# S5 state inputs in four PSUM banks of their own, computed two pairs ahead, and streamed tiles in two banks

## The reference

```
bu_re = einsum('blgc,gnc->blgn', uf, bbar_re)      # 32 groups of 16 channels -> 64 states each
bu_im = einsum('blgc,gnc->blgn', uf, bbar_im)
_, _, s_re, s_im = lax.associative_scan(_complex_affine_combine, (abar_re, abar_im, bu_re, bu_im), axis=1)
y = einsum('blgn,gcn->blgc', s_re, c_re) - einsum('blgn,gcn->blgc', s_im, c_im) + d * uf
...
merged = gates[0] * (y_rw @ w_branch[0]) + gates[1] * (y_s5 @ w_branch[1]) + gates[2] * (y_gla @ w_branch[2])
```

## Time and profile before

| | us |
|---|---|
| median of 3 runs | 1868.67 |
| lowest, highest | 1866.36, 1868.9 |
| profiled execution | 1868.79 |
| its span | 1866.7 |
| TensorE busy in the span | 1766.2 (95%) |
| VectorE busy | 907.7 (49%) |
| ScalarE, GpSimd busy | 406.8, 295.9 |
| mean granted TensorE clock | 0.979 of full speed |

### The profile page before, as it was taken

How to read it: one execution, slowest core, us unless ns; L and a number is a source line. 1 busy time by engine, 2 the same in 40 slices (tenths; PEclk the granted TensorE clock), 3 DMA queues, 4 the chain that set the end, 5 groups by cost and what they waited for, 6 DMA issues and landing times.

```text
span 1866.7 us, 25902 instructions
## 1 busy us (share of the span) xinstructions
PE 1766.2 (95%) x10456; PEld 1393.1 (75%) x10456; DVE 907.7 (49%) x1725; ACT 406.8 (22%) x771; POOL 295.9 (16%) x305
## 2 busy tenths in 40 slices
PE   7999999899999999899899999988999899999997
PEld 5434454488888888656899996856798688888886
DVE  1247542464675444575587643187711432255511
ACT  1312453221012210346222002221421101200000
POOL 0100252122002211005233110066000000000000
PEclk9999999999999999999999999889999999999999
DMA  7775492122233222321345454232312343244443
GB/s 290 290 294 200 159 346 107 68 86 76 110 135 113 90 78 82 111 68 48 133 167 173 164 179 140 92 110 106 114 55 84 118 153 135 91 158 157 142 152 113
DMA packets 38703, 256.22 MB, mean 137 GB/s; under 512 B 4128, under 2 KB 7328, under 8 KB 9024
## 3 DMA queue, kind: packets, MB, share of 16 engines
q1 hardware_dynamic: 36240, 240.86, 36.6%
q0 software_dynamic: 1776, 9.57, 1.4%
q10 hardware_dynamic: 576, 4.19, 0.5%
HBM read 247.27 MB, written 7.34 MB: 136 GB/s over the span
## 4 chain that ended last, share of the span: by engine, by line
PE 80%; DVE 12%; ACT 2%; issue 2%; POOL 2%; DMA 2%; SPq 0%; ACTq 0%; DVEq 0%; POOLq 0%
PE ps L595 79%; DVE arena L1873 1%; PE ps L790 1%; DMA ring<-weights 1%; DVE arena L2031 1%; DMA xT<-x_t 1%; POOL aux L1676 0%; DVE aux L1903 0%; DVE arena L1904 0%; DVE arena L1905 0%; ACT hT L1322 0%; DVE arena L2070 0%; POOL aux L1659 0%; DVE spare L2143 0%; POOL hT L1719 0%
## 5 line engine op out<-in xcount | busy, mean ns | idle before, releaser
L595 PE MATMUL ps<-hT,ring 128*128 128x256 f32 (+3 forms) x3184 | 744.1, 392 | 22.6 <-issue 17.0
L595 PEld LDWEIGHTS ps<-hT,ring 128*128 128x128 f32 (+1 forms) x3184 | 574.6, 194 | 182.3 <-issue 112.6
L595 PE MATMUL ps<-arena,ring 128*128 128x256 f32 (+3 forms) x1884 | 380.4, 358 | 5.0 <-DVE arena L1905 3.2
L595 PEld LDWEIGHTS ps<-arena,ring 128*128 128x128 f32 (+1 forms) x1884 | 317.6, 190 | 59.0 <-issue 13.7
L1659 POOL TENSOR_TENSOR aux<-aux 128x256 f32<-128x256 f32 (+1 forms) x46 | 50.1, 1088 | 611.0 <-ACT aux L1257 542.9
L595 PE MATMUL ps<-arena,sums 128*128 128x256 f32 (+1 forms) x768 | 136.5, 327 | 1.3 <-DVE aux L1969 1.3
L595 PEld LDWEIGHTS ps<-arena,sums 128*128 128x128 f32 x768 | 118.2, 191 | 12.3 <-DVE aux L1969 2.5
L1257 ACT ACTIVATE aux<-xT 128x256 f32<-128x256 f32 (+1 forms) x64 | 30.9, 494 | 285.7 <-DVE xT L2061 93.3
L1676 POOL TENSOR_SCALAR aux<-aux,small 128x512 f32<-128x512 f32 (+1 forms) x48 | 70.9, 1485 | 113.6 <-DVE small L1921 113.4
L1695 POOL TENSOR_TENSOR arena<-arena 128x256 f32<-128x256 f32 (+1 forms) x32 | 27.0, 843 | 332.6 <-ACT arena L1442 332.6
L595 PE MATMUL ps<-hT,sums 128*128 128x128 f32 (+1 forms) x512 | 78.6, 302 | 0.7 <-DVE aux L1969 0.4
(11 more groups left out here) (335 smaller groups left out, 1817.1 us busy)
## 6 DMA issues: line engine op xcount, KB each, us to landing
ring<-weights SPq DMA_DIRECT2D x224, 1024.0 KB, 4.9
kept_turns<-aux ACTq DMA_DIRECT2D x4, 1024.0 KB, 5.6
arena<-kept_turns POOLq DMA_DIRECT2D x6, 512.0 KB, 4.9
kept_keys_values<-spare POOLq DMA_DIRECT2D x1, 2048.0 KB, 10.2
arena<-kept_keys_values POOLq DMA_DIRECT2D x1, 2048.0 KB, 8.2
tab<-tables SPq DMA_DIRECT2D x1, 1344.0 KB, 13.7
arena<-mem_t SPq DMA_DIRECT2D x2, 512.0 KB, 5.6
xT<-ctx_t SPq DMA_DIRECT2D x1, 1024.0 KB, 9.2
```

Of the source, the lines that this page charges most:

```text
L595: ins = nc.tensor.matmul(o_, lhsT, rhs, start=start, stop=stop, skip_group_check=True)
```

## The change

Only TensorE's program differs. The inputs `("bu", n)` are opened from a new pool `state` of banks 0 to 3: even pairs get banks 0 and 1, odd pairs banks 2 and 3. From `s5_in(0)` to the loop's end, everything else from the pool `run` (the two GLA outputs, `glago` 3, the rw tiles and three gate tiles) takes turns in banks 4 and 7. `s5_in(1)` stands ahead of the loop; inside, `s5_in(m + 2)` comes right behind `s5_out(m)`. After the loop `run` has six banks again, in another order.

```diff
-            turn = {"run": 0, "hold": 0, "mod": 0}
-            pools = {"run": [0, 1, 2, 3, 4], "hold": [5, 6], "mod": [7]}
+            turn = {"run": 0, "hold": 0, "mod": 0, "state": 0}
+            pools = {"run": [0, 1, 2, 3, 4], "hold": [5, 6], "mod": [7], "state": [0, 1, 2, 3]}
...
-                    open_bank(("bu", n))
+                    open_bank(("bu", n), "state")
...
+            pools["run"], turn["run"] = [4, 7], 0
             s5_in(0)
             taken(pe, ("gatt",))
...
+            s5_in(1)
             for m in range(S5T // 2):
-                if m + 1 < S5T // 2:
-                    s5_in(m + 1)
                 s5_filler(2 * m)
                 s5_out(m)
+                if m + 2 < S5T // 2:
+                    s5_in(m + 2)
                 s5_filler(2 * m + 1)
+            pools["run"] = [4, 7, 0, 1, 2, 3]
```

## The result

The changed kernel takes 1871.1 us (median of 18 runs, 1867.66 to 1874.42), the kernel before 1867.17 (18 runs, 1863.45 to 1871.73). The ratio is 1.0018 with a 95% interval of 1.0010 to 1.0025: +3.4 us, from 1.9 to 4.7. The forecast was 1870.6 within 1867.5 to 1874.0, and no change beyond 0.2% as the likeliest. The profiled execution has a span of 1869.2 us, 2.5 above the one before. The profiled executions are not equally typical: that of the kernel before (1868.79 us) lies 1.6 us above its median of 18, that of the changed kernel (1871.29) 0.2 above.

The account below looks back on a forecast made before the run. The S5 loop was taken as bound by a ring of states, rw tile 7 and VectorE, not by inputs; +0.6 at `s5_in(0)` and +1.15 at rw tile 13 gave +1.8, 1870.6 us, range 1867.5 to 1874.0.

Parts of the forecast that it names:

- either long idle time: TensorE's idle times ahead of `s5_out(2)` and `s5_out(4)`, forecast to stay near 7.8 and 5.8 us.
- rival C: Rw tile 3's addition misses its gap between GpSimd's operations, tile 4's is then unblocked: +0.4 us, 1869.2 us; chance 0.13.
- The waits for rw tiles 7 and 11: VectorE's waits for these tiles in the S5 loop, forecast to grow from 4.2 to 5.3 us.
- rival B: Low clock lasts longer behind the two restarts, with narrow `s5_in` first: +3.9 us, 1872.7 us; chance 0.25.
- 1.54 us at `s5_out(7)`: TensorE's idle time ahead of `s5_out(7)`, forecast to grow from 0.3 to about 1.5 us.
- the ring: The S5 loop's limit: states, then rw tile 7, then VectorE, then states; inputs computed earlier gain 0.
- Rival D: Inputs were the S5 loop's limit, so both long idle times vanish: -19 us, about 1850 us; chance 0.07.
- Wait of `s5_in(0)`, +0.6: `s5_in(0)` waits for bank 1 until ScalarE has read `glago` 2: +0.6 us, bounds 0.5 and 0.9.
- Place of `s5_in`: `s5_in` ahead of the odd rw tile: odd tiles end 1.06 us later, costing only +1.15 us at rw tile 13.
- my term: Cost of moving `s5_in` ahead of the odd rw tiles, all of it at rw tile 13: +1.15 us.
- The giving back behind rw tile 11: Rw tile 11 comes 1.06 us later, but tile 12's addition still ends at 1290.1: cost 0.
- the loss at rw tile 13: Rw tile 13's addition is held by GpSimd's operation and ends at 1295.4 instead of 1294.24: +1.15 us.

Follow-up runs that it names:

- the banks alone: Against the kernel before: only the changed banks (inputs in 0 to 3, everything streamed in 4 and 7), TensorE's order as before; 1867.13 us, ratio 0.9997.
- `s5_in(0)` without its wait: The changed kernel with the four input banks in the order 2, 3, 0, 1; 1868.97 us, ratio 0.9998 to the kernel before.
- the kernels with the added matmuls: Changed banks plus 12 and 10 overwritten wide matmuls ahead of `s5_out(2)` and `s5_out(4)`: order of before 1863.81 us, order of the change 1869.63 us.
- the order alone: Against the kernel before: only the changed order of `s5_in`, all banks from the one pool of six; 1870.35 us, ratio 1.0011.
- fastest kernel with separate banks: Changed kernel with both streamed tiles ahead of `s5_out`, input banks 2, 3, 0, 1, and 6 and 5 wide matmuls added; 1856.44 us, ratio 0.9930.
- both streamed tiles ahead: The kernel before with both streamed tiles of a pair moved ahead of `s5_out(m)`; 1857.43 us, ratio 0.9949.

## Why the prediction came out right

The number came out right, and part of that is luck. Of the signs that the prediction set itself, several failed. It said that it was wrong if either long idle time shrank by over 2 us: the one at `s5_out(2)` shrank by 4.95. The additions of rw tiles 3 and 4 took 0.42 us each, where 3.1 us gone was to mean rival C. The waits for rw tiles 7 and 11 were to grow to 5.3 us and were 4.11 and 6.46. Behind the second restart the clock was not back within 6 us, which was to mean rival B: the work there took 4.0 us longer than at full clock, so the low clock lasted about 8 us, against 5.5 before (both worked out from the rows' lengths). What held: 0.6 us at `s5_in(0)`, no wait of a streamed tile for a bank, 1.54 us at `s5_out(7)`, and the inputs no part of the ring.

**What bounds the loop: right.** But for tile 2's, the inputs were never waited for, and computing them earlier gave nothing; moving the rw tiles gave 9.5 us where moving the inputs cost time. Rival D was wrong for the reason given; the idle time that did shrink did so through the additions, not through the inputs.

**Wait of `s5_in(0)`, +0.6: right in length, too small in price.** 0.56 us of idle time. That it can keep the clock low for longer in the GLA outputs, 1.7 us more, was not in the sum. Of the +1.83 us in the first row of the table, 0.63 is the later start of `s5_in(0)` (0.56 of it idle time) and 1.53 the clock, less 0.33 us of a wait that I missed: before, `s5_in(1)` needed bank 3, which VectorE freed late; in the change it does not (VectorE's wait for it is 0.93 us, not 1.31). I had looked at the place of `s5_in(1)` and not at its banks.

**Additions against GpSimd: the mechanism right, the tile wrong.** I had rival C hang on rw tile 3. It was rw tile 2: with tile 2's input 0.4 us earlier relative to it, its addition met GpSimd's second operation and took 1.32 us instead of 0.48. Everything behind moved later by 0.9 us, so that the additions of rw tiles 3 and 4 were not blocked (0.42 each, for 1.48 and 3.13). It gives -2.2 us up to `s5_out(2)`. The pattern 1.32, 0.42, 0.42 stands in the profiles of the changed kernel, of the banks alone and of `s5_in(0)` without its wait, and not where the six banks are shared. The stretch to `s5_out(2)` is 29.7 to 29.8 us in these three and in the kernel with `s5_in` ahead of `s5_out`, and 31.95 before. No run moves the input of tile 2 by itself, so the way from it to the additions is read from the rows and not tested. The banks gave 2.2 us in the profiles where I had put 0, with a chance of 0.13 for 1.4.

**Place of `s5_in`: the steps right, the clock too small.** At full clock it is 1.07 us per odd tile (forecast 1.06). I let the clock cost nothing in it; at low clock it is 1.97. Against the banks alone the order costs 3.3 us in the profiles, where my term was 1.15: 2.6 us behind `s5_out(4)`, and 0.74 at the first restart, where I had it all given back. There I let rw tile 8's addition go ahead of GpSimd's next operation. It came 0.01 us behind and took 1.53 us; the kernels with the added matmuls show the same tie and the same loss (the addition from 1262.72 behind GpSimd's from 1262.71 took 1.53 us, and the stretch up to `s5_out(4)` is 0.93 us longer than in the order of before). The giving back behind rw tile 11 happened (2.28 us late there, 1.15 one tile later) and so did the loss at rw tile 13 (from 1.15 to 2.5 us late, 1.35 for my 1.15). Rival B was therefore no rival but a part: its term, 1.06 us, is real at the second restart, where it measured 1.2. At the first one it did not appear in the changed kernel: the place cost 1.04 us there (the table's middle row), and the low clock cost about 1.7 us of work against 2.8 before.

**The sum.** +1.8 forecast, +2.5 between the two profiled spans, +3.4 (1.9 to 4.7) in the timed runs. The size came out near because misses cancel: 2.2 us gained by the additions and 0.3 by the bank of `s5_in(1)`, 1.5 and 1.2 us lost to the clock. The first loss appears in four of six profiles with the wait, so even that sum is one outcome of two. The range was needed: 1871.1 is 0.5 us above the forecast, and the ratio, 1.0018, is closer to the limit of 0.2% than to my 1.0010. The stretches give 2.0 us and the timed runs 3.4. The gap is within the interval, and part of it is that the profiled execution of before was itself a slower one than its median.

## What to carry to other kernels

Before giving a buffer of its own to something, look whether anybody waits for that thing; here every long wait was for another tile, and swapping two calls in the order of the program gave 9.5 us where four PSUM banks gave nothing. Where TensorE restarts at low clock, put what the others wait for directly behind the restart, since what stands ahead of it there costs about twice (1.97 us for 1.07). A new wait of half a microsecond can be worth more than its length where work at low clock follows, and in a loop of engines that block each other a shift of 0.4 us came with a gain of 2 us in the profiles, so forecasts of about 1 us need a range of several.

## What the runs showed of the hardware that I had not expected

- TensorE's clock went to its lower level, 1.2 GHz, in a stretch in which it was busy without a break, behind matmuls of 64 rows and 64 columns (mean granted clock 0.79 from `s5_in(0)` to `s5_in(1)`; 0.86 with one wide tile between the two halves).
- With an idle time of 0.56 us ahead of that stretch it was 1.7 us longer in four of six profiles and not at all in two. The outcome has two values, 28.5 and 30.2 us, with nothing between.
- In the loop, idle times of up to 1.89 us were not followed by low clock and those of 2.58 us and more were. In between it went either way: ahead of `s5_out(4)`, 2.24 us in the fastest kernel with separate banks were followed by it, and 2.23 us in the same kernel with the wide tile between the GLA outputs were not; the 2.15 us of the changed kernel ahead of `s5_out(1)` were. Wide matmuls whose result nobody reads kept the clock up (6.96 us from `s5_out(4)` to the odd tile's addition for 10.42).
- An addition on VectorE with both inputs in SBUF and a GpSimd operation of 128x512 hold each other up, and 0.01 us decides who is first. At 1230.43 VectorE's addition started and took 0.42 us, and GpSimd's operation from 1230.44 took 1.55 instead of 1.27. At 1261.17 GpSimd started, and the addition from 1261.18 took 1.53.
- The longest such hold-ups, 3.12 to 3.36 us, were additions that began while GpSimd was issuing DMAs and had its next operations directly behind: rw tile 4 before (the DMAs from 1231.38 to 1232.50, the addition from 1232.18) and in the order alone, rw tile 8 in the kernel with `s5_in(0)` without its wait and in the same with added matmuls. An addition that began 0.03 us into the same DMAs took 0.43 us (1229.28, both streamed tiles ahead). What parts the two cases is not shown.
